# Four modulation pieces ahead of the first projection, the rest inside the attention core

## What is computed

```python
m = silu(c) @ mod_w[l] + mod_b[l]          # six parts of 1024: sh_a, sc_a, g_a, sh_f, sc_f, g_f
h = x * (1 + sc_a) + sh_a
x = layer_norm(ALPHA * x + g_a * mix(h))   # attention, short convolution, recurrent scan, merged
h = x * (1 + sc_f) + sh_f
x = layer_norm(ALPHA * x + g_f * experts(h))
```

## Time and profile before

| | us |
|---|---|
| runs of the kernel | 7156.51, 7157.47, 7167.98 |
| median | 7157.47 |
| span of the profiled execution | 7157.4 |
| start, to the next stage's first ACT work | 138.86 |
| attention core, layer 0 (1384 to 1598) | 214 |
| first norm, layer 0 (1787 to 1872) | 85 |

### The profile page before, as it was taken

One profiled execution on the slowest core, in us unless ns is written; L12 is line 12 of the kernel. 1 busy time (PEld: TensorE's weight loads), 2 busy tenths in 40 slices (PEclk: granted clock), 3 DMA queues, 4 the chain that ended last, 5 costly groups with the idle time before them and its releaser, 6 DMA issues. The chain is left out here.

```text
span 7157.4 us, 97855 instructions
## 1 busy us (share of the span) xinstructions
PE 5719.2 (80%) x37784; PEld 4035.7 (56%) x37784; DVE 4104.1 (57%) x8602; ACT 1924.0 (27%) x3637; POOL 2759.7 (39%) x2928
## 2 busy tenths in 40 slices
PE   4877999879488787878788789997875778878876
PEld 3865999859333333333367669996673333333332
DVE  2276432264677777776635482424546677767776
ACT  1356211141122222222225452112312222222221
POOL 0211000010277777777602200001005777777774
PEclk8999999999799999999989899998988999999998
DMA  5100222102799999999930111210158999999998
GB/s 225 43 34 20 75 80 75 49 21 87 303 408 407 404 407 405 406 404 407 395 145 9 41 52 67 75 71 25 49 208 311 406 407 404 405 406 402 409 399 324
DMA packets 424148, 1658.80 MB, mean 232 GB/s; under 512 B 48136, under 2 KB 67272, under 8 KB 409420
## 3 DMA queue, kind: packets, MB, share of 16 engines
q0 software_dynamic: 368640, 1342.34, 47.3%
q1 hardware_dynamic: 53598, 304.86, 11.2%
q10 hardware_dynamic: 1440, 5.24, 0.2%
HBM read 1637.40 MB, written 17.48 MB: 231 GB/s over the span
## 5 line engine op out<-in xcount | busy, mean ns | idle before, releaser
L1797 PE MATMUL ex_ps_y<-early,peer_small 128*128 128x512 f32 x5120 | 2393.6, 614 | 750.3 <-DMA early<-in_peer_v,ex_index 749.7
L1797 PEld LDWEIGHTS ex_ps_y<-early,peer_small 128*128 128x128 f32 x5120 | 943.5, 193 | 2120.0 <-DMA early<-in_peer_v,ex_index 1265.4
L1680 DVE CUSTOM_DVE_ANT_0 ring<-ring,ex_ps_h 128x1024 f32<-128x1024 f32 x1280 | 1519.1, 1218 | 819.9 <-DMA ring<-in_peer_u,ex_index 804.9
L1555 POOL DMA_INDIRECT ring<-in_peer_u,ex_index x1280 | 1220.4, 953 | 759.8 <-issue 295.9
L1555 POOL DMA_INDIRECT early<-in_peer_v,ex_index x1280 | 1225.3, 957 | 424.9 <-issue 375.5
L1750 ACT ACTIVATE peer_small<-ident,ex_w 128x128 f32<-128x128 f32 x1280 | 448.2, 393 | 953.0 <-PE ex_ps_y L1797 953.0
L738 POOL TENSOR_TENSOR att_qs<-att_q,ring 128x512 f32<-128x512 f32 x16 | 20.2, 1264 | 1108.8 <-DMA att_lam_in<-in_lam 951.8
L237 PE MATMUL conv_ps<-h_high,conv_wh 128*128 128x320 f32 x1024 | 318.5, 311 | 8.2 <-DVE conv_wl L135 8.2
L1740 ACT ACTIVATE ex_act<-ex_dot 128x16 f32<-128x16 f32 x80 | 17.3, 216 | 1137.5 <-DVE ex_dot L1680 1137.5
L237 PE MATMUL conv_ps<-h_low,conv_wh 128*128 128x320 f32 x1024 | 318.3, 311 | 0.0
L237 PE MATMUL conv_ps<-h_high,conv_wl 128*128 128x320 f32 x1024 | 318.1, 311 | 0.0
(11 more groups left out here) (326 smaller groups left out, 12311.7 us busy)
## 6 DMA issues: line engine op xcount, KB each, us to landing
ring<-in_w_in SPq DMA_DIRECT2D x54, 2048.0 KB, 8.0
ring<-in_mod_w SPq DMA_DIRECT2D x16, 2048.0 KB, 15.7
ring<-in_w_branch SPq DMA_DIRECT2D x12, 2048.0 KB, 8.1
early<-in_mod_w SPq DMA_DIRECT2D x12, 2048.0 KB, 19.4
ring<-in_peer_u,ex_index POOLq DMA_INDIRECT x1280, 8.9
early<-in_peer_v,ex_index POOLq DMA_INDIRECT x1280, 9.0
mod_w<-in_mod_w SPq DMA_DIRECT2D x8, 2048.0 KB, 25.1
room<-in_peer_wq SPq DMA_DIRECT2D x16, 1024.0 KB, 16.2
```

Source lines behind the costliest of these rows:

```text
L1555: nc.gpsimd.indirect_dma_start(rows[slot], None, table, bass.IndirectOffsetOnAxis(ap=index[n % 4][:, s:s + 1], axis=0)).then_inc(arrived[s ...
L1680: V.tensor_tensor_reduce(out=row, in0=row, in1=ps_h[:], scale=1.0, scalar=0.0, op0=ALU.mult, op1=ALU.add, accum_out=dot[n % 2][:, s:s + 1] ...
L1797: last = nc.tensor.matmul(ps_y[n % 2][:, c:c + 512], diag[s % DIAGS], v_row[s % V_SLOTS][:, c:c + 512], start=s == 0, stop=s == TOPK - 1)
```

## The change

- `prepare`, `modulation` and `modulate_and_transpose` become one stage, `begin`. It loads four pieces (parts 0 and 1 of layer 0) into four buffers, some of which are rooms used later, and keeps the silu of the conditioning vectors in HBM (`mod_silu`).
- The other eight pieces of a layer and the first four of the next are multiplied in `attention_core`, one in the third and one in the fifth block of heads 0 to 5, all through `ring[0]` and one corner of the rotation's PSUM bank. A new wait stands before each piece on PE (weights) and on DVE (bias, matmuls), and SP's list gets, for each piece, a load of weights, a load of bias and a store. The next stage's first weights come into `ring[0]` behind the last piece.
- `first_norm` and `MixerEnd.finish` lose their pieces.
- `mod_rows` is stored with 32 rows per group of columns, by one DMA per piece; a part is read back (`mod_row`, `by_piece`) as 8 rows of 512 bytes per partition.

```diff
-                for i in range(2):
-                    sp.dma_start(bufs[i][:], mod_weights(T, l, i)).then_inc(w_loaded[i], 16)
-                mod.load_small(sp, T, l, zeroed, small_in)
-                for i in range(2, MOD_CHUNKS):
...
-                mod.store(sp, T, l, summed, rows_out)
...
+FIRST_CHUNKS = 2 * D // CHUNK
...
+def mod_row(T, l, cond, part):
+
+    per = D // P
+    return T["mod_rows"][bass.ds(l, 1), per * part:per * (part + 1), cond].to_broadcast([P, per, P])
...
+def mod_multiply(nc, out, csilu, weights):
+
+    for k in range(KT):
         for g in range(MOD_GROUPS):
...
+            last = nc.tensor.matmul(out[32 * g:32 * (g + 1), :], csilu[:, k, :], weights[:, k, g * P:(g + 1) * P], start=k == 0, stop=k == KT - 1)
+    return last
...
+def begin(nc, T, h_split, ident, ring, main, room):
...
+                sp.dma_start(cond[:], T["cond"]).then_inc(cond_in, 16)
+                sp.dma_start(bufs[0], mod_weights(T, slice(0, 1), 0)).then_inc(w_loaded[0], 16)
+                sp.dma_start(lb_in[:], T["rec_lb"].rearrange("j d n -> d j n")).then_inc(lb_loaded, 16)
+                sp.dma_start(sel[:], T["sel"][0:2, :]).then_inc(lb_loaded, 16)
+                for i in range(1, FIRST_CHUNKS):
+                    sp.dma_start(bufs[i], mod_weights(T, slice(0, 1), i)).then_inc(w_loaded[i], 16)
+                sp.dma_start(pieces[:], mod_bias(T, slice(0, 1), 0, FIRST_CHUNKS)).then_inc(bias_in, 16)
+                sp.dma_start(ident[:], T["ident"]).then_inc(copied, 16)
+                for b in range(NB):
+                    src = T["x_sample"][b * P:(b + 1) * P, :] if b < NB - 1 else T["x_prompt"]
+                    sp.dma_start(xb[b], src).then_inc(x_in, 16)
+                sp.wait_ge(silu_done, 1)
+                sp.dma_start(T["mod_silu"], csilu[:]).then_inc(rows_out, 16)
+                sp.wait_ge(summed, 1)
+                sp.dma_start(mod_out(T, slice(0, 1), 0, FIRST_CHUNKS), pieces[:]).then_inc(rows_out, 16)
+                sp.wait_ge(rows_out, 32)
+                for c in range(2):
+                    for j in range(2):
+                        sp.dma_start(by_piece(vec[:, c, j, :]), mod_row(T, 0, c, j)).then_inc(vec_in, 16)
+                sp.dma_start(ring[0][:], T["w_first"][0]).then_inc(first_in, 16)
+                sp.wait_ge(lb_ready, 1)
...
 def attention_core(nc, l, T, q_t, k_t, v_tok, o_tok, ring, ident):
...
+        MOD_UNITS = (2, BLOCKS - 1)
...
+                sp.dma_start(csilu[:], T["mod_silu"]).then_inc(silu_in, 16)
+
+                def store_piece(i):
+                    sp.wait_ge(mod_summed, i + 1)
+                    sp.dma_start(mod_out(T, *piece_place(i)), pieces[i % 2][:].unsqueeze(1)).then_inc(mod_stored[i % 2], 16)
+
+                for i in range(MOD_CHUNKS):
+                    if i:
+                        sp.wait_ge(mod_done, i)
+                    sp.dma_start(ring[0][:], mod_weights(T, *piece_place(i))).then_inc(mod_in, 16)
+                    if i:
+                        store_piece(i - 1)
+                    if i >= 2:
+                        sp.wait_ge(mod_stored[i % 2], 16 * (i // 2))
+                    sp.dma_start(pieces[i % 2][:].unsqueeze(1), mod_bias(T, *piece_place(i))).then_inc(bias_in, 16)
+                sp.wait_ge(mod_done, MOD_CHUNKS)
                 sp.dma_start(ring[0][:], w_in(T, l, ZG)).then_inc(k_out, 16)
...
+                def modulate(n):
+                    i = piece_at(n)
+                    if i == 0:
+                        pe.wait_ge(silu_in, 16)
+                    pe.wait_ge(mod_in, 16 * (i + 1))
+                    pe.wait_ge(rot_used, 2 * min(where(n)[0] + 2, HEADS))
+                    if i:
+                        pe.wait_ge(mod_summed, i)
+                    mod_multiply(nc, ps_rot[:, 0:P], csilu, ring[0]).then_inc(mod_done, 1)
...
                     if n:
                         values(n - 1)
+                    if piece_at(n) is not None:
+                        modulate(n)
                     turn(n)
...
+                def take_piece(i):
+                    dve.wait_ge(bias_in, 16 * (i + 1))
+                    dve.wait_ge(mod_done, i + 1)
+                    V.tensor_tensor(pieces[i % 2][:], ps_rot[:, 0:P], pieces[i % 2][:], ALU.add).then_inc(mod_summed, 1)
...
                     if n:
                         store(n - 1)
+                    if piece_at(n) is not None:
+                        take_piece(piece_at(n))
...
 def first_norm(nc, l, T, y_tok, x_tok, gb, h_tok, h_split, x_to, ident):
...
-                pe.wait_ge(silu_done, 1)
-                for i in range(4):
-                    chunk(i)
                 for b in range(NB):
                     turn(b)
-                    chunk(4 + b)
-                for i in range(4 + NB, MOD_CHUNKS):
-                    chunk(i)
...
-                dve.wait_ge(tile_done, MOD_CHUNKS)
-                mod.add_bias(summed)
...
-        prepare(nc, T, ident)
-        modulation(nc, slice(0, 1), T, ring)
-        modulate_and_transpose(nc, 0, T, rows, h_split, ident, 0, ring)
+        begin(nc, T, h_split, ident, ring, main, rooms)
```

More of the change, by code:

```diff
@@ L327 @@
 MOD_GROUPS = 4
[L330 to L376, removed]
@@ L379, in mod_weights, with mod_bias @@
+FIRST_CHUNKS = 2 * D // CHUNK
 def mod_weights(T, l, i):
     return T["mod_w"][l, i].rearrange("a p k n -> (a p) k n")
-def modulation(nc, l, T, ring):
-    with ExitStack() as ctx:
[L387 to L391, removed]
+def mod_bias(T, l, i, n=1):
+    return T["mod_b"][l, i:i + n].rearrange("a i p n -> p (a i) n")
@@ L404, in _ @@
+                sp.wait_ge(first_in, 16)
+                sp.wait_ge(lb_out, 16)
+                sp.wait_ge(copied, 48)
             @block.gpsimd
             def _(pool):
-                mod.clear(pool, zeroed)
+                nc.gpsimd.memset(csilu[:], 0.0).then_inc(zeroed, 1)
             @block.scalar
             def _(act):
-                mod.silu(act, small_in, silu_done)
+                act.wait_ge(zeroed, 1)
+                act.wait_ge(cond_in, 16)
+                act.activation(csilu[:, :, 0:2], cond[:], ACT.Silu).then_inc(silu_done, 1)
@@ L414, in _ @@
                 pe.wait_ge(silu_done, 1)
[L415 to L420, removed]
-                dve.wait_ge(tile_done, MOD_CHUNKS)
-                mod.add_bias(summed)
[L425 to L444, removed]
-                for b in range(NB):
[L446 to L469, removed]
@@ L640, in attention_core, with piece_at, pieces_before, piece_place @@
         ps_o = ctx.enter_context(nc.psum_tensor("att_ps_o", [P, 512], F32))
+        csilu, pieces = sb("att_csilu", [P, KT, 32]), [sb(f"att_piece{j}", [P, P]) for j in range(2)]
+        MOD_UNITS = (2, BLOCKS - 1)
         def where(n):
             return n // BLOCKS, n % BLOCKS
+        def piece_at(n):
+            h, u = where(n)
+            i = len(MOD_UNITS) * h + MOD_UNITS.index(u) if u in MOD_UNITS else MOD_CHUNKS
+            return i if i < MOD_CHUNKS else None
+        def pieces_before(n):
+            return sum(piece_at(m) is not None for m in range(n))
+        def piece_place(i):
+            return (bass.ds(l, 1), i + FIRST_CHUNKS) if i + FIRST_CHUNKS < MOD_CHUNKS else (bass.ds(l + 1, 1), i + FIRST_CHUNKS - MOD_CHUNKS)
         def keys_of(n):
@@ L960, with load_last @@
     names = (*NormBeside.names, "gate", "residual")
-    def load_last(self, gate, gate_rows, turn, residual, x_rows, products, ring, mod_rows, output):
+    def load_last(self, gate, gate_rows, turn, residual, x_rows, products):
         self.gate, self.gate_rows, self.turn = gate, gate_rows, turn
         self.residual, self.x_rows, self.products = residual, x_rows, products
-        self.ring, self.mod_rows, self.output = ring, mod_rows, output
     def finish(self, sp):
@@ L974, in finish @@
             sp.dma_start(self.residual[:, b, :], self.x_rows(b)).then_inc(done, 16)
-        for i in range(2):
-            sp.wait_ge(self.low_done, self.split_of(self.output + i))
-            sp.dma_start(self.ring[i][:], self.mod_rows(i)).then_inc(done, 16)
-        sp.wait_ge(done, 16 * (NB + 2))
+        sp.wait_ge(done, 16 * NB)
 def attention_out(nc, l, T, h_split, o_tok, sig, merged_t, y_tok, x_tok, rows, ring, ident):
```

176 lines of the change are left out of this document (93 added, 83 removed).

## The result

The changed kernel takes **7220.5 us** (median of 4 runs, 7215.9 to 7228.2), beside 7159.1 for the kernel before: ratio 1.008, 95% interval 1.0068 to 1.0092. The profiled execution took 7223.8 us, with a span of 7222.1. The forecast was 7054 (7030 to 7088): wrong in sign, and 167 us off.

What follows compares the result with a forecast made beforehand. No engine was taken as the bound; barriers set the time stage by stage. Start -69, first norms -66, attention cores +28 and experts' ends +4 gave -103, so 7157.4 became 7054 us, range 7030 to 7088.

Steps and rivals of the forecast that it cites:

- Price of a 512-byte row: Vector loads: 30 ns per row, 46 at most, so 4096 rows on 16 engines take 7.7 us against 5.1 before.
- Joined start, -69: Start of the kernel: vectors land at 45.5 us, next stage at 68.5 to 69; gain 69 us (60 to 73).
- three signs that I named for being wrong: Core growing over 30 us per layer, start's vectors landing after 55, or experts' end shifting by 8 or more.
- First norm, -33 per layer: First norm without modulation pieces ends at 1839 instead of 1872.06: 33 us saved per layer, 66 in all (62 to 67).
- Experts' end, +2 per layer: Last vectors amid gathers: 2.6 us added DMA work less 0.8 slack, +2 per layer, +4 in all (0 to 20).
- rival (c): Short rows are starved by gathers at the experts' end: 16 us more, 7070; chance 0.10.
- My lower bound: Experts' end: short rows aren't starved beside gathers, so the vectors land no later than before.
- Gates at nothing: Gate loads in short rows, issued stages ahead of use, cost nothing; 2.6 us each where that cover failed.
- Attention core, +14 per layer: Twelve pieces per layer: +0.4 at third block, 2.0 at fifth, 2.4 per head; +28 us for twelve heads (10 to 50).
- rival (a): Attention core: added matmuls keep the clock up, so the pieces cost about 14 us instead of 28, 7040; chance 0.12.
- rival (b): Attention core: PE falls to half clock waiting for weights, pieces take 3.21 us; 31 more, 7085; chance 0.15.
- rival (d): Attention core at half clock throughout: 87 us more per layer, 7200, slower than before; chance 0.02.

Runs made afterwards that it cites:

- e4: Changed kernel with the eight shared 512-byte rows of a vector 640 bytes apart instead of 16 KB; 7550.8 us, ratio 0.988 to the kernel before.
- e3: Changed kernel with 33 instead of 32 slots per group, so a vector's shared short rows lie 16.5 KB apart; 7563.5 us, ratio 0.990 to the kernel before.
- e11: Changed kernel with the eight shared short rows of a vector 1 KB apart instead of 16 KB; 7538.8 us, kernel before 7578.5.
- e1: Changed kernel with the modulation table laid out so each partition reads a vector as one 4 KB row; ratio 0.9865 to the kernel before.
- e7: e1 with each piece's weights in the attention core loaded in two halves of 1 MB; ratio 0.9828 to the kernel before.
- e5: The changed kernel itself, run again unaltered on another chip as control; ratio 1.008 to the kernel before.
- e2: Changed kernel with each partition reading its own 512-byte rows, from the bias table (values not the computed ones); 7559.3 us, 0.989 of the kernel before.
- e12: Changed kernel with each partition reading own 512-byte rows of the modulation weights, all multiples of 16 KB apart; 7517.5 us, ratio 0.992 to the kernel before.
- e8: Changed kernel with the eight shared short rows of a vector 8 KB apart instead of 16 KB; 7712.1 us, ratio 1.014 to the kernel before.
- e9: Changed kernel with the eight shared short rows of a vector 4 KB apart instead of 16 KB; 7624.7 us, kernel before 7578.5.
- e6: Kernel before with only the changed kernel's modulation table layout and its read in 512-byte rows 16 KB apart; ratio 1.0242 to the kernel before.

## Why the prediction was wrong

**The step that failed is "Price of a 512-byte row".** I priced a row by the DMA engine's time for packets of that size (30 ns, 46 at most) from rows of other reads the earlier trace rows, and gave that bound to everything. None of them was a read of eight rows 16 KB apart by every partition. For rows at harmless distances the price was right: in e4 3442 packets took 107.6% of 16 engines from 38 to 44 us, 30 ns each, and where the places differ (e3, e4, e11) the short rows cost 0.8 to 2.3 us more than long ones in the start, forecast 2.6. But the bound was no bound: in the changed kernel a packet took 90 ns, and the engines were still idle for more than half of the time. By the upper price I put the vectors at 53 (46 ns on 4096 rows give 49.6; the 53 does not follow from it), 16 to 19 us after their issue, and they took 42.5.

*Joined start, -69.* The structure was right to 2.5 us: e1's vectors are used at 43.6 and e3's, in short rows, at 46.1 (forecast 45.5), and e1 comes to 66.5. With the slow read it is 99.6: 30 us of the gain lost. Of the three signs that I named for being wrong, vectors after 55 and an experts' end later by 8 came; a core longer by 30 did not.

*First norm, -33 per layer.* Right in e1: -33.8. With the slow read -3.7. I wrote that the vectors "may land 2.6 us later". With the rows at a harmless distance that much is hidden (50.2 us in e3 and e4). With the slow read DVE's 14.8 us of work over it did not cover it, and a wait of 30 us stood at the stage's beginning.

*Experts' end, +2 per layer.* Wrong twice. With clean distances it is +14 at use (e3: 28.9 us from issue to use in layer 0, 14.9 in the earlier trace rows): rival (c), the starved short rows, came true in its time, and its 10 on the path was a little low. On top of it the distance adds 20, 33.9 together in layer 0. My lower bound, the 1 KB rows that got 696 packets against 19 gathers, came from a stretch with hardly any gathers.

*Gates at nothing.* Right: between core and first norm the changed kernel took 190.8 us, e1 with its fast reads 189.6, the kernel before 187.5. The 2 us that both have, no run explains.

*Attention core, +14 per layer.* +16.3 and +17.2: right to 2 or 3 us, less than the first core's scatter. So was its split: +0.4 at the third block, the fifth block late by its weights, which e7 shows by taking the wait away. Some of that closeness is luck, since two rivals that I had set apart are each half there and work against each other. Of rival (a): the transposes of the fourth block, which took 1.27 us in five heads of the kernel before, take 0.76 or 0.77 in all heads. Of rival (b): the piece behind the DMA wait loses the clock half a microsecond in (3.21 us), the other does not (1.95); the wait itself passes at 1.00, so the piece does not start cold, as rival (b) had it, but becomes slow on its way. The granted clock over the core is 0.90, before 0.87; rival (d) fell.

*Sum.* e1 comes near the forecast's 7054 (7062, interval 7045 to 7079), but it reads long rows, and my sum was for short ones. The kernels with short rows at harmless distances, e3 and e4, show 7087 and 7075 (a single run each), the most of it the experts' ends. The 160 us that e5 has over e1 are the read of the vectors: in the start, the two first norms and the two experts' ends. The earlier trace rows showed stages that wait for these loads, and I moved the loads' form and looked only at its count.

The Trainium skill, DMA: Bandwidth & Descriptors, Specifications, has 512 bytes as enough for the full rate. e2, e4, e11 and e12 agree, within 1.6 us of the long rows on 2 MB; e8, e9 and the changed kernel, with the same 512 bytes, take 3.5 to 5.8 times as long, so the size of a row alone does not decide, and here the measurement does.

Shown: layout alone makes the loss; neither sharing nor coinciding addresses does it alone, both together do; for shared rows the modulus acts like 8 KB. Only inferred: that one place of the memory serves its readers one after another, and e12 says that this is not the whole of it. Not tried: own rows within some 100 KB; several copies of each row, read by different partitions.

## What to carry to other kernels

When a change alters how a small table is read back by all partitions, look at the addresses, not only at bytes and descriptors: eight shared rows 2, 4, 8 or 16 KB apart took 2.1 to 5.8 times as long as long rows, and half a KB of padding or one contiguous row removes most or all of it. A price from other transfers' packets is no bound for a read from other addresses. A slow load also holds up whatever ordinary load is queued behind it, and the profile then names that one; and a load that goes out amid gathers should have few, long rows.

## Unexpected of the hardware

- 2 MB in 4096 rows of 512 bytes: 9.4 us from own rows, 9.4 from eight shared rows 640 bytes apart, 49.5 from eight shared rows 8 KB apart; in the changed kernel some 40 GB/s with the engines 44% busy.
- Such reads also slow the issuing queue: four issues took 18.68 us instead of 1.75, and in e6 four token loads behind them 18.40 instead of 2.32. It takes no slow read for that: behind 8 MB of weights at the changed kernel's start, four token loads took 17.48 us to issue (from 5.22).
- Beside gathers that fill the engines, 4096 short rows take 28.9 us from issue to use, 512 long ones 15.8.
- The changed kernel took 226 us longer for an experts' stage on another chip, and within 2 us the same for the start, the first core and the first norm.
